# Half of K of six pairs of output chunks in the two output projections as Strassen-Winograd blocks, and the low parts of the weights in two halves each

## The reference

```python
def pool_layer(x, norm_g, w_in, w_group, scale, w_out):
    uz = rmsnorm(x, norm_g) @ w_in
    u, z = uz[..., :2048], uz[..., 2048:]
    pooled = causal_window_mean(u) - u              # windows 2, 4, 8, 16
    mixed = einsum('bsgc,gcd->bsgd', pooled, w_group) * scale
    y = mixed * silu(z)
    return x + y @ w_out                            # K = 2048, 1024 outputs

def mla_layer(x, ...):
    ...
    o = causal_mla_attention(q_nope, q_rope, k_nope, k_rope, v)   # 16 heads of 128
    y = o.reshape(B, S, 2048) * silu(z)
    return x + y @ w_out                            # K = 2048, 1024 outputs
```

## Time and profile before

| what | value |
|---|---|
| time, median of three runs | 1304.52 us |
| smallest and largest of the three | 1303.99 and 1305.34 us |
| time of the profiled execution | 1304.71 us |
| span of its records | 1303.0 us |
| TensorE matmuls | 1293.0 us busy, 99%, 6826 instructions |
| TensorE weight loads | 1093.0 us, 84% |
| VectorE | 826.7 us, 63%, 1200 instructions |
| ScalarE | 586.1 us, 45%, 976 instructions |
| GpSimd | 454.0 us, 35%, 208 instructions |
| chain of work that ended last | 95% of it on TensorE |
| TensorE's granted clock | full in each of 40 slices of the span |

### The profile page before, as it was taken

How to read it: one execution, slowest core, us unless ns; L and a number is a source line. 1 busy time by engine, 2 the same in 40 slices (tenths; PEclk the granted TensorE clock), 3 DMA queues, 4 the chain that set the end, 5 groups by cost and what they waited for, 6 DMA issues and landing times.

```text
span 1303.0 us, 17714 instructions
## 1 busy us (share of the span) xinstructions
PE 1293.0 (99%) x6826; PEld 1093.0 (84%) x6826; DVE 826.7 (63%) x1200; ACT 586.1 (45%) x976; POOL 454.0 (35%) x208
## 2 busy tenths in 40 slices
PE   9999999999999999999999999999999999999998
PEld 7888888888778888888888787898879999998886
DVE  7999728233292466665434575567989999985442
ACT  5224323222333466656633345568464444443223
POOL 2444544444444442452544342323430000015441
PEclk9999999999999999999999999999999999999999
DMA  4333423333723422226143345433323223323331
GB/s 163 97 97 105 128 83 97 97 97 97 274 81 97 129 65 82 82 64 212 49 161 97 114 146 153 125 104 124 96 67 130 98 99 113 114 83 112 113 95 67
DMA packets 47870, 143.60 MB, mean 110 GB/s; under 512 B 6032, under 2 KB 6032, under 8 KB 47024
## 3 DMA queue, kind: packets, MB, share of 16 engines
q1 hardware_dynamic: 43984, 129.88, 32.0%
q10 hardware_dynamic: 3808, 12.64, 2.7%
HBM read 121.46 MB, written 10.49 MB: 101 GB/s over the span
## 4 chain that ended last, share of the span: by engine, by line
PE 95%; ACT 1%; DVE 1%; issue 1%; DMA 1%; POOL 0%; SPq 0%; POOLq 0%; ACTq 0%
PE bank L1867 30%; PE bank L1869 30%; PE bank L1868 30%; PE bank L2039 2%; PE bank L2028 1%; PE bank L2029 1%; DMA x<-x_in 1%; PE bank L1891 0%; POOL w_lo L624 0%; DVE zv L1600 0%; ACT f_prob_t L871 0%; PE bank L2354 0%; PE bank L2184 0%; PE bank L2185 0%; ACT pool_xg L718 0%
## 5 line engine op out<-in xcount | busy, mean ns | idle before, releaser
L624 POOL TENSOR_TENSOR w_lo<-raw,w_hi 128x1024 fp32r<-128x1024 f32 (+1 forms) x146 | 359.7, 2467 | 543.9 <-ACT w_hi L692 543.7
L692 ACT ACTIVATE w_hi<-raw 128x1024 fp32r<-128x1024 f32 x149 | 156.2, 1054 | 233.7 <-PE bank L1869 183.3
L669 POOL TENSOR_TENSOR w_lo<-raw,w_hi 128x1024 fp32r<-128x1024 f32 x22 | 53.5, 2437 | 263.3 <-DVE w_lo L1724 204.7
L1867 PE MATMUL bank<-y_hi,w_hi 128*128 128x512 f32 x256 | 101.5, 396 | 0.0
L1868 PE MATMUL bank<-y_lo,w_hi 128*128 128x512 f32 x256 | 101.3, 396 | 0.0
L1869 PE MATMUL bank<-y_hi,w_lo 128*128 128x512 f32 x256 | 101.2, 395 | 0.0
L1867 PE MATMUL bank<-pool_xg,w_hi 128*128 128x512 f32 x248 | 98.5, 397 | 0.2 <-POOL w_lo L624 0.2
L1868 PE MATMUL bank<-pool_xg,w_hi 128*128 128x512 f32 x248 | 98.1, 396 | 0.0
L1869 PE MATMUL bank<-pool_xg,w_lo 128*128 128x512 f32 x248 | 98.1, 395 | 0.0
L1867 PE MATMUL bank<-right,w_hi 128*128 128x256 f32 x336 | 94.4, 281 | 0.0
L1869 PE MATMUL bank<-right,w_lo 128*128 128x256 f32 x336 | 94.1, 280 | 0.0
(11 more groups left out here) (410 smaller groups left out, 3549.0 us busy)
## 6 DMA issues: line engine op xcount, KB each, us to landing
raw<-stream SPq DMA_DIRECT2D x187, 512.0 KB, 3.6
raw_x<-stream SPq DMA_DIRECT2D x18, 512.0 KB, 4.7
spill<-x ACTq DMA_DIRECT2D x2, 2048.0 KB, 6.8
xg_spill<-mla_xg ACTq DMA_DIRECT2D x2, 2048.0 KB, 11.9
rope_q<-turned_hl SPq DMA_DIRECT2D x64, 64.0 KB, 2.5
zx<-xg_spill SPq DMA_DIRECT2D x2, 1536.0 KB, 8.6
stacked<-fq SPq DMA_DIRECT2D x24, 128.0 KB
stacked<-fk SPq DMA_DIRECT2D x24, 128.0 KB
```

What stands on the lines that cost most here:

```text
L624: pool.tensor_tensor(w_lo[:, j % RING, 0:width], raw[:, j % RAW, 0:width], plain(w_hi[:, j % RING, 0:width]), ALU.subtract).then_inc(tile_ ...
L669: pool.tensor_tensor(w_lo[:, s, 0:D], raw[:, d % RAW, 0:D], plain(w_hi[:, s, 0:D]), ALU.subtract).then_inc(tile_lo, 1)
L692: act.activation(w_hi[:, t % RING, 0:width], raw[:, t % RAW, 0:width], ACT.Copy).then_inc(tile_hi, 1)
L1867: pe.matmul(target, a_hi, b_hi, start=start, stop=False)
```

## The change

**Which products.** The eight output chunks keep the first half of K (chunks 0 to 7 of y) as tiles of eight blocks, called `first`. Of the second half of K, outputs 6 and 7 are done as before (`second`). Outputs (0, 1), (2, 3) and (4, 5) are done by seven products a pair, in both projections, so six pairs in all. A product has four chunks of K by 256 tokens by 128 outputs. Its operands are blocks of y or of w, or sums of two to four of them. The weights of a pair come in two tiles, `direct` and `crossed`, whose blocks are laid out so that a sum of 1024 columns and two of 512 give the four weight sums. The stage still has 16 tiles, in another order: `first` 0 to 4 (tiles 0 to 4), the first pair (5 and 6), `first` 5 (tile 7), the second pair (8 and 9), `first` 6 (10), the third pair (11 and 12), `second` 6, `first` 7, `second` 7. 48 matmuls of 512 columns a pair become 84 of 256 columns.

**Right operands.** When all of y is there, VectorE makes four sums of blocks of `z` (T1 to T4, 1024 columns each, `out_t`), the low parts of y's second half in two operations of 2048 columns, and the low parts of the four T. ScalarE makes the four T high parts (`out_t_hi`) behind y's own. In the attention layer `product_low` and its semaphore are gone with that; the last head's y is now made before the low parts.

**Weights' sums.** For each pair VectorE sums the raw tiles (1024, 512 and 512 columns), ScalarE casts the two results (`out_w_hi`), VectorE cuts them (`out_w_lo`). SyncE may load the tiles that overwrite the pair's raw tiles only after these sums (`out_loads`: tiles 7 and 8 after the first pair's, 10 and 11 after the second's, 13 and 14 after the third's).

**Banks.** A pair's four banks are c, a, b and d. ScalarE copies the half of c that holds the first product out (`copy_first`) before TensorE may write c's other half with the fourth product. VectorE adds the rest to `x` (`combine`, seven operations). TensorE begins pair 0 once VectorE has taken the first bank of `first` tiles (`bank_taken`), and pairs 1 and 2 once `x_ready` tells that the pair before is combined.

**Norm chunks.** ScalarE squares chunks 0 and 1 behind the split of tile 10 and chunks 2 and 3 behind that of tile 13, and multiplies by the gain only three splits later. `mla_sq` and `mix_sq` move in memory.

**GpSimd.** Every `w_lo` is cut by two operations of half the columns, in the whole kernel. The semaphore `tile_lo` is signalled after the second.

**Names.** New semaphores share the counters of old ones, and in the rows below they have the old names: `pooled_ready` counts T sums, `pooled_hi_done` and `pooled_lo_done` T high and low parts, `angle_ready` weight sums, `table_done` and `pos_in` their high and low parts, `in_evac` the products that are through, `z_silu` the copies, `patterns` the banks taken.

The core of the difference:

```diff
+OUT_TILES = (*(("first", m) for m in range(5)), ("direct", 0), ("crossed", 0), ("first", 5), ("direct", 1), ("crossed", 1),
+             ("first", 6), ("direct", 2), ("crossed", 2), ("second", 6), ("first", 7), ("second", 7))
+OUT_PAIRS = 3
+FIRST_BANK = (0, 1, 2, 3, 4, 1, 6, 7)
+CELL_BANKS = ((5, 6, 7, 0), (2, 3, 4, 5), (0, 1, 5, 2))
...
+def out_blocks(kind, i):
+
+    if kind in ("first", "second"):
+        return [(k + HALF_K * (kind == "second"), i) for k in range(HALF_K)]
+    rows = (2, 3) if kind == "direct" else (3, 2)
+    return [(4 * r + c, 2 * i + n) for n, r in enumerate(rows) for c in range(4)]
...
+            def out_loads(stage):
+
+                for j in range(7, len(OUT_TILES) - 1):
+                    kind, i = OUT_TILES[j - RAW]
+                    if kind in ("direct", "crossed"):
+                        sp.wait_ge(out_summed, OUT_SUMMED + OUT_SUMS * (out_pair(stage, i) + 1))
+                    load(0, TILE[stage] + j)
+
...
-                    pool.tensor_tensor(w_lo[:, j % RING, 0:width], raw[:, j % RAW, 0:width], plain(w_hi[:, j % RING, 0:width]),
-                                       ALU.subtract).then_inc(tile_lo, 1)
+                    for c in (slice(0, width // 2), slice(width // 2, width)):
+                        low = pool.tensor_tensor(w_lo[:, j % RING, c], raw[:, j % RAW, c], plain(w_hi[:, j % RING, c]), ALU.subtract)
+                    low.then_inc(tile_lo, 1)
...
+                def weight_casts(i):
+                    p = out_pair(stage, i)
+                    act.wait_ge(out_summed, OUT_SUMMED + OUT_SUMS * (p + 1))
+                    act.wait_ge(out_product_done, PRODUCT_DONE + OUT_SIGNALS * p)
+                    for r in range(2):
+                        act.activation(out_w_hi[:, r, :], out_sums[:, r, :], ACT.Copy).then_inc(out_cast, 1)
+
+                def copy_first(i):
+                    if i:
+                        act.wait_ge(n.x_ready, 2 * i)
+                    p = out_pair(stage, i)
+                    act.wait_ge(out_product_done, PRODUCT_DONE + OUT_SIGNALS * p + 1)
+                    act.activation(out_parts[:, 0, :], cells(stage, i)[0][:, TOKENS[0]], ACT.Copy, scale=-1.0).then_inc(first_copied, 1)
+
+                if first == 0:
+                    split_tile(stage, 0, 0)
+                done = 4 * (stage == "mla_out")
+                for i, t in enumerate(T_ORDER):
+                    act.wait_ge(t_summed, T_SUMMED + done + i + 1)
+                    act.activation(out_t_hi[:, t], out_t[:, t], ACT.Copy).then_inc(t_cast, 1)
+                for k in range(1, PC):
                     split_tile(stage, 0, k)
-                    if k >= 3 and k % 2:
-                        norm_chunk((k - 3) // 2)
-                norm_chunk(DC - 1)
+                    if k in (5, 8, 11):
+                        copy_first((k - 5) // 3)
+                    if k in (3, 7, 10):
+                        weight_casts((3, 7, 10).index(k))
+                    if k in (7, 10):
+                        first_chunk = 2 * (k == 10)
+                        square(first_chunk)
+                        square(first_chunk + 1)
...
-                for k in range(DC + 1):
-                    if k < DC:
-                        take_bank(stage, n, k)
-                    if k:
-                        norm_chunk(n, k - 1, xg_hi, xg_lo, gain, [(sqsum[:], lambda c: sq[:, c % 2, :])])
...
+            def right_operands(stage, ready, y_count):
...
+                dve.wait_ge(ready, PC)
+                dve.tensor_tensor(t1, b12, b11, ALU.subtract).then_inc(t_summed, 1)
+                dve.wait_ge(t_summed, T_SUMMED + done + 1)
+                dve.tensor_tensor(t2, b22, t1, ALU.subtract).then_inc(t_summed, 1)
...
+                y_block_low(2)
+                t_block_low(3)
+                y_block_low(3)
+                t_block_low(1)
+                t_block_low(2)
+                t_block_low(0)
...
+                def take(m):
+                    dve.wait_ge(tile_used, TILE[stage] + OUT_AT["first", m] + 1)
+                    dve.tensor_tensor(x[:, m, :], out_bank(stage, FIRST_BANK[m])[:], x[:, m, :], ALU.add).then_inc(bank_taken, 1)
...
+                def weight_sums(i):
+                    p, t = out_pair(stage, i), TILE[stage] + OUT_AT["direct", i]
+                    for u in (t, t + 1):
+                        dve.wait_ge(tile_loaded[u % RAW], 16 * (u // RAW + 1))
+                    dve.wait_ge(out_cut, OUT_CUT + 2 * p)
+                    direct, crossed = raw[:, t % RAW, 0:D], raw[:, (t + 1) % RAW, 0:D]
+                    dve.tensor_tensor(halves(out_sums[:, 1, :]), halves(direct), both(crossed[:, HALF_D:D]), ALU.add).then_inc(out_summed, 1)
+                    dve.wait_ge(out_summed, OUT_SUMMED + OUT_SUMS * p + 1)
+                    dve.tensor_tensor(out_sums[:, 0, HALF_D:D], out_sums[:, 1, HALF_D:D], direct[:, 0:HALF_D], ALU.add).then_inc(out_summed, 1)
+                    dve.wait_ge(out_summed, OUT_SUMMED + OUT_SUMS * p + 2)
...
+                def combine(i):
...
+                    dve.wait_ge(bank_taken, BANK_TAKEN + 2 * out_pair(stage, 0) + m + 2)
+                    dve.wait_ge(first_copied, FIRST_COPIED + p + 1)
+                    dve.wait_ge(out_product_done, product + 2)
+                    settle(dve.tensor_tensor(u2, c[:, TOKENS[1]], out_parts[:, 0, :], ALU.add))
+                    dve.wait_ge(out_product_done, product + 3)
+                    settle(dve.tensor_tensor(x[:, m, :], b[:], x[:, m, :], ALU.add))
...
+                    dve.tensor_tensor(x[:, m + 1, :], a[:], x[:, m + 1, :], ALU.add).then_inc(n.x_ready, 1)
...
+                weight_sums(0)
+                for m in range(3):
+                    take(m)
+                weight_lows(0)
+                take(3)
+                take(4)
+                weight_sums(1)
+                combine(0)
+                weight_lows(1)
+                total(0)
+                total(1)
+                take(5)
+                weight_sums(2)
+                combine(1)
+                weight_lows(2)
+                total(2)
+                total(3)
+                combine(2)
...
-                if h == HEADS - 1:
-                    product_low(range(8, 14))
...
+                wait_tile(0, t)
+                pe.wait_ge(t_cut, cuts + 1)
+                half_k_product(c, 0, direct, 0, y_block(2, 0), out_product_done)
+                pe.wait_ge(t_cut, cuts + 2)
+                half_k_product(a, 0, direct, 1, t_block(3), tile_used)
+                wait_tile(0, t + 1)
+                pe.wait_ge(t_cut, cuts + 3)
+                half_k_product(b, 0, crossed, 0, y_block(3, 0), tile_used)
+                pe.wait_ge(out_cut, OUT_CUT + 2 * p + 1)
+                pe.wait_ge(t_cut, cuts + 4)
+                pe.wait_ge(first_copied, FIRST_COPIED + p + 1)
+                half_k_product(c, 1, sums_42, 1, t_block(1), out_product_done)
+                half_k_product(b, 1, sums_42, 0, y_block(3, 1), out_product_done)
+                pe.wait_ge(out_cut, OUT_CUT + 2 * p + 2)
+                pe.wait_ge(t_cut, cuts + 5)
+                half_k_product(d, 0, sums_31, 0, t_block(2), out_product_done)
+                pe.wait_ge(t_cut, cuts + 6)
+                half_k_product(a, 1, sums_31, 1, t_block(0), out_product_done)
...
+            def out_product(stage, n, first=0):
+
+                taken = BANK_TAKEN + 2 * out_pair(stage, 0)
+                for j, (kind, i) in enumerate(OUT_TILES):
+                    if (kind, i) == ("first", 4) and stage == "pool_out":
+                        pe.wait_ge(y_ready, PC)
+                    if kind == "direct":
+                        pe.wait_ge(bank_taken, taken + (1, 5, 6)[i])
+                        if i:
+                            pe.wait_ge(n.x_ready, 2 * i)
+                        out_seven(stage, i)
+                    elif kind != "crossed" and j >= first:
+                        if (kind, i) == ("first", 5):
+                            pe.wait_ge(bank_taken, taken + 2)
+                        elif (kind, i) == ("first", 6):
+                            pe.wait_ge(n.x_ready, 2)
+                        out_tile(stage, j, range(8))
```

199 lines of the change are left out of this document (149 added, 50 removed).

## The result

The changed kernel takes **1311.91 us** (median of six runs, 1311.02 to 1313.31) where the kernel before, run beside it, takes 1304.76 (1303.99 to 1305.42). The ratio is 1.0057, with a 95% interval of 1.0047 to 1.0068: 7.15 us slower, in the forecast direction, inside the range of 1304 to 1324, and about half of the 13.3 us that were forecast. The profiled execution took 1312.98 us with a span of 1311.3.

The account below looks back on a forecast made before the run. TensorE, busy 99% of the span, bounds the kernel. 1304.7 - 7.4 (matmuls) - 0.15 (old wait) + 20.0 (waits) + 0.9 (GpSimd's halves) = 1318 us; range 1304 to 1324, the forecast's own band 1312 to 1324 (chance 0.63).

Parts of the forecast that it names:

- Matmuls saved: Both output projections: seven products of 256-column matmuls save 1.23 us a pair, 7.4 us for six pairs.
- the old wait: Attention projection: TensorE's existing wait of 0.15 us before tile 1 goes, with product_low.
- rival D: The blocks don't save: 256-column matmuls with waits between products lose the 1.23 us a pair; 1325 us, chance 0.04.
- The rule of the two engines: VectorE operations with both inputs in SBUF wait for GpSimd's; with both queued they alternate, so their times add.
- rival B: Half the waits: attention's first wait and the second-block waits stay, ScalarE's copies hide; 1307 to 1311 us, chance 0.14.
- the signs that were to show the forecast right: TensorE idle 15 to 24 us more, named releasers, y_lo 2.2 unheld, out_sums and out_t often 2.4, pool stage 93 us.
- The waits: New TensorE waits in both projections: 7.4 us in pool and 12.6 in attention, together 20.0 us.
- Part 1: Operands at a stage's start: VectorE's 17.1 us plus GpSimd's tiles delay the first block, 0.2 us pool, 3.3 attention.
- Part 2: Ring behind the first block: sums, loads, splits and combine make TensorE wait for copies and later blocks, 0.5 to 2.8 each.
- GpSimd's halves elsewhere: Outside the projections: halved low parts cost TensorE 0.9 us, at its one wait for GpSimd.
- Rival A: Cover holds: VectorE's chain is hidden, 0 to 2 us of waits; 1297 to 1299 us, chance 0.14.
- Rival C: Waits of 3 us lower TensorE's clock: 2.5 us per half-level stretch, +10 after four waits, 1328 us; chance 0.05.

Follow-up runs that it names:

- e9: e6's orders plus, on VectorE, the first pair's weight sums ahead of two T low parts, against the changed kernel: 1305.31 us.
- e2: Changed kernel with GpSimd's low parts in one operation of 1024 columns again instead of two halves: 1311.81 us.
- e1: Kernel before with only GpSimd's low parts cut in two halves, projections unchanged: 1305.26 us.
- e10: e9 with VectorE's combine(2), last bank and its low part ahead of sums of squares, and ScalarE's gain multiplications earlier, at the attention projection's end: 1304.16 us.
- e3: Changed kernel with VectorE's take(0) moved ahead of the last three T low parts and the weight sums: 1311.37 us.
- e4: Changed kernel with ScalarE's copy of the first product placed right behind the weight casts of its pair: 1309.57 us.
- e6: Changed kernel with take(0) earlier, ScalarE's casts of pairs 2 and 3 and all copies earlier, and combine ahead of the next pair's weight sums: 1308.14 us.
- e11: e10 with GpSimd's low parts in one operation of 1024 columns: 1305.06 us.
- e12: e10 with TensorE's two mean products moved behind the mixer's second tile, qk_tile(1): 1304.85 us.

## Why the prediction was right, and where its sizes were off

**Matmuls saved: 7.4 forecast.** e9's stages without their one wait are 86.01 and 80.46 us, against 89.65 and, without the 0.15 of the old wait, 84.02: 3.64 and 3.56, together 7.2. Right; rival D is out.

**The rule of the two engines: right.** In the rows above they go in turn, and neither has two turns running. GpSimd's second half never passed VectorE, and e2 shows that the grain changes nothing. The Trainium skill (SBUF — State Buffer, Who interferes with whom) gives the lock to "whoever issues first", which it says of VectorE's two-port modes, and leaves open who goes next when both have work queued.

**The band.** 1311.91 is 0.1 under the 1312 at which the forecast's own band begins, and 0.9 over the upper end of rival B, half the waits. The size is nearer to B than to 1318. B's account did not come, though: it has ScalarE's copies hidden, and in the attention stage they stayed (1.49, 1.71 and 1.77 us). Of the signs that were to show the forecast right, out_t and out_sums at 2.3 us, the unheld y_lo at 2.29 and the releasers came. Two did not: TensorE is idle 12.3 us more by the page and not 15 to 24, and the pool stage lasts 90.0 us and not 93.

**The waits: 20.0 forecast, 12.8 measured.** This is the term that was mis-sized, and its 7.2 us are more than the 6.1 by which 1318 was too high. From TensorE's starts beyond its pace:

| wait | pool: forecast, measured | attention: forecast, measured |
|---|---|---|
| first block | 0.2, 0 | 3.3, 2.25 |
| its copy | 1.4, 0.27 | 1.4, 1.49 |
| second block | 2.8, 1.88 | 2.8, 1.89 |
| its copy | 1.0, 0.45 | 2.3, 1.71 |
| third block | 1.0, 0.45 | 0.5, 0 |
| its copy | 1.0, 0.65 | 2.3, 1.77 |
| sum | 7.4, 3.7 | 12.6, 9.1 |

Ten of the twelve stand where they were forecast, with the releasers that were named. Nine of the ten were forecast 0.3 to 1.1 us too long, one 0.1 too short. The 0.5 for the attention stage's third block doesn't follow from the terms beside it (VectorE's x at D + 17.5, TensorE there at D + 17.9, so no wait), and none was measured. The traces show three reasons for the rest:
- *Part 1, the time inserted by GpSimd.* For the attention stage three tiles at 2.53 were counted, 7.6. The chain from the last `z` (done at 654.59) to the bank taken (678.36) is 23.8 us. Less the 17.1 counted for VectorE's own work, that leaves 6.7: six halves that cost 1.1 each. In the pool stage it is 25.9 us (z done at 235.95, bank taken at 261.83), where 27.2 were counted.
- *Where TensorE stood.* It came to the first block at 263.0 and 676.2, and not at 262.45 and 674.8. Ahead of both lay the later start (+0.55), ahead of the second also the pool stage (+0.37) and the stretch behind it (+0.23); the `z` that opens each chain slid by as much. In the pool stage the bank is taken 1.2 us ahead of need, so the sums, the loads and the copy are early too: 0.27 for 1.4.
- *Part 2, the sums with GpSimd's halves between them.* 5.1 was counted for pair 1 (2.6 and 2.5); it took 4.6, because the first sum of 1024 columns had started before GpSimd's half:

```profile
688.79 1.22 DVE L1372 TENSOR_TENSOR out_sums<-raw 128x1024 f32<-128x1024 f32 x1 [5.76 <-issue]
690.05 1.67 DVE L1374 TENSOR_TENSOR out_sums<-out_sums,raw 128x512 f32<-128x512 f32 x1
691.75 1.67 DVE L1376 TENSOR_TENSOR out_sums<-out_sums,raw 128x512 f32<-128x512 f32 x1
...
696.76 0.68 DVE L1401 TENSOR_TENSOR x<-bank,x 128x512 f32<-128x512 f32 x1
```

The combination ended at 697.44, 19.0 us behind the first block's start (19.8 forecast), and TensorE had used 17.2 of them (17.0). A difference of two long chains carries the errors of both: 0.8 and 0.2 in 19 made 1.9 of 2.8.

**GpSimd's halves elsewhere: 0.9 forecast, 0.6 measured** (e1, e2).

**The sum.** The stages changed by +0.37 and +5.83 us, where the forecast had +3.7 and +8.8 (-3.7 and the waits, and the old 0.15). With 0.55 at the start and 1.5 spread over stretches that the change doesn't touch, the span grew by 8.3; the median, 1.1 below the profiled execution, by 7.15.

**Rival A** was not far: e9 and e10 have 86.0 and 81.0 us in the projections. But it would not have given its 1297 to 1299, since both it and my sum took the work behind the stage for free: "free" was true only because TensorE's own waits lengthened the attention stage. Without them VectorE is 6 us late at its end (e9), and 4.8 to 5.6 of the 6.8 us saved go to the mixer, 1.7 of them by the clock.

**Rival C, the falling clock,** was given 0.05 and as an extra of 10 us. The changed kernel's profile has no fall in its stages. The others have ten: one in the projections of e2, one in e3 and three in e4, and one in the mixer of e6, e9, e10, e11 and e12, each at a wait of 2.2 to 3.9 us. Nine last 3.4 us and cost about 1.7, where matmuls fill them, and e6's lasts 6.8. Two waits of over 2 us have none: 2.25 us in the changed kernel and 2.07 in e6. Every wait of over 2.3 us has one. So the rival's condition, waits of 3 us, was sound, and 0.05 was low for it: the forecast's own waits of 2.8 and 3.3 us were of that size, and they came out shorter, so that in leaving the clock out the sum had luck. The rival's price of 2.5 us was too high, and a fall just ahead of another wait of the ring cost nothing (e2, e3).

Executions of one kernel differ too: the mean granted clock of e10's eleven runs from 0.996 in the slowest (1305.68 us) to 1.000 in the fastest (1303.19). Three of the changed kernel's six have 0.998 where the profiled one has 0.999, so that a fall in those is possible, and not shown. The row at 0.50 in e3 agrees with the Trainium skill (TensorE: Matmul & The Clock Gate, HAM oscillation), which warns that a pause for data costs once more in the matmuls behind it.

**What stays open.** Why the clock fell behind e2's and e4's waits of 2.2 to 2.3 us and not behind the same wait in the changed kernel. Why the view names no releaser ("issue") for the second blocks; the times fit VectorE's last `x` of the pair before. Whether the mixer's chain could be made shorter, and the change then pay, was not tried.

## What to carry to other kernels

A saving in matmuls pays only if every engine that prepares its operands keeps up; look for the operation on which a ring of buffers hangs (here the first weight sums) and put it ahead of what is less urgent: from e6 to e9 that took 3.9 us off the attention stage. Where VectorE (two inputs in SBUF) and GpSimd both have work queued, add their times. When stalls are removed, look at what they had covered: VectorE's sums behind the stage were hidden by TensorE's waits, and took back most of what the better order won. And look at the granted clock behind every wait that is left: a fall made the one in e10 half as dear again.

## What the runs showed of the hardware that I had not expected

- Operations of GpSimd (1.29 us alone) and VectorE (1.22) with both inputs in SBUF alternate strictly over six turns and more, each pair taking 2.25 to 2.3 us; halving GpSimd's operations changes nothing (stage 89.95 and 90.00 us).
- A wait of TensorE can cost a second time: at ten waits of 2.2 to 3.9 us (e2, e3, e4, e6, e9 to e12) its clock was granted at half, for 3.4 us and once 6.8, about 1.7 us lost where matmuls filled the 3.4; behind 2.25 us in the changed kernel it stayed at full, and behind 2.28 us in e2 it did not.
- Such a loss need not show in the time: e2 has a fall in its attention stage, the changed kernel none, and the stage lasts 89.95 and 90.00 us.
